# Down projections of both feed-forward parts with activations stationary and 512 weight columns moving

## What is computed

```python
# first block, end
h = rmsnorm(x, g_pre_mlp)
f = square(relu(h @ w_up))          # 2048 -> 8192
f = f @ w_down                      # 8192 -> 2048
x = x + rmsnorm(f, g_post_mlp)
# second block: mixers, cross attention, then
u = rmsnorm_2(h, ffn_norm_w)
h = h + square(relu(u @ ffn_w1)) @ ffn_w2
return rmsnorm_2(h, final_norm_w)   # x * rsqrt(mean(x*x) + 1e-6) * w, per token
```

## Time and profile before

| | us |
|---|---|
| median of three runs | 2883.87 |
| lowest, highest | 2883.01, 2886.10 |
| the profiled execution | 2884.09 |
| its span, first to last instruction | 2882.3 |

### The profile page before, as it was taken

How to read it: one execution, slowest core, us unless ns; L and a number is a source line. 1 busy time by engine, 2 the same in 40 slices (tenths; PEclk the granted TensorE clock), 3 DMA queues, 4 the chain that set the end, 5 groups by cost and what they waited for, 6 DMA issues and landing times.

```text
span 2882.3 us, 51300 instructions
## 1 busy us (share of the span) xinstructions
PE 2807.8 (97%) x19504; PEld 2458.9 (85%) x19504; DVE 2005.7 (70%) x2465; ACT 1440.9 (50%) x1867; POOL 158.3 (5%) x173
## 2 busy tenths in 40 slices
PE   9999999999999999999998999889989999999998
PEld 8888888888888888888787888788878888888887
DVE  7888887768647566575887667855877666575665
ACT  6545556566444444445656437434654444444444
POOL 0000000230000000001000000131220000000001
PEclk9999999999999999999999999999999999999999
DMA  7565554756666666656464434402536665656664
GB/s 245 175 194 163 169 175 152 231 176 208 189 188 188 190 188 187 188 184 194 133 196 118 133 111 125 125 4 75 183 118 207 189 188 189 190 186 189 187 189 139
DMA packets 482034, 486.70 MB, mean 169 GB/s; under 512 B 14945, under 2 KB 479841, under 8 KB 481873
## 3 DMA queue, kind: packets, MB, share of 16 engines
q1 hardware_dynamic: 480288, 478.55, 53.7%
q0 software_dynamic: 1584, 5.93, 0.6%
HBM read 481.28 MB, written 3.15 MB: 168 GB/s over the span
## 4 chain that ended last, share of the span: by engine, by line
PE 88%; DVE 7%; ACT 3%; issue 2%; DMA 0%; SPq 0%; DVEq 0%; ACTq 0%
PE pg L430 53%; PE pg L437 28%; DVE lo L348 1%; PE p L1082 1%; DVE work L795 1%; PE p L1099 1%; DVE xa L656 1%; ACT hi L310 1%; PE p L1510 0%; PE pg L1780 0%; DMA resid<-x 0%; DVE work L773 0%; PE p L1259 0%; PE p L1102 0%; PE p L1077 0%
## 5 line engine op out<-in xcount | busy, mean ns | idle before, releaser
L348 DVE TENSOR_TENSOR lo<-raw,hi 128x1024 fp32r<-128x1024 f32 x895 | 1086.3, 1232 | 646.2 <-ACT hi L310 640.0
L310 ACT ACTIVATE hi<-raw 128x1024 fp32r<-128x1024 f32 x894 | 939.0, 1059 | 1128.7 <-PE pg L437 1064.4
L430 PE MATMUL pg<-xa,hi 128*128 128x512 f32 x4224 | 1070.6, 395 | 7.2 <-DVE xa L656 3.8
L430 PEld LDWEIGHTS pg<-xa,hi 128*128 128x128 f32 x4224 | 761.7, 189 | 149.5 <-issue 6.3
L430 PE MATMUL pg<-xb,hi 128*128 128x512 f32 x3004 | 755.5, 393 | 3.8 <-ACT hi L310 1.9
L430 PEld LDWEIGHTS pg<-xb,hi 128*128 128x128 f32 x3004 | 541.3, 189 | 102.8 <-issue 2.9
L437 PEld LDWEIGHTS pg<-xa,lo 128*128 128x128 f32 x4224 | 576.3, 191 | 52.8 <-DVE lo L348 11.1
L437 PE MATMUL pg<-xa,lo 128*128 128x256 f32 x4224 | 591.6, 283 | 5.5 <-DVE lo L348 4.7
L437 PEld LDWEIGHTS pg<-xb,lo 128*128 128x128 f32 x3004 | 409.5, 190 | 34.1 <-DVE lo L348 5.1
L437 PE MATMUL pg<-xb,lo 128*128 128x256 f32 x3004 | 419.4, 282 | 3.0 <-DVE lo L348 3.0
L320 ACT ACTIVATE half<-pg 128x512 f32<-128x512 f32 x220 | 128.6, 585 | 77.5 <-PE pg L437 70.9
(11 more groups left out here) (422 smaller groups left out, 1681.1 us busy)
## 6 DMA issues: line engine op xcount, KB each, us to landing
raw<-w_in SPq DMA_DIRECT2D x264, 512.0 KB, 4.5
raw<-ffn_w SPq DMA_DIRECT2D x256, 512.0 KB, 4.3
raw<-w_up SPq DMA_DIRECT2D x128, 512.0 KB, 3.9
raw<-w_down SPq DMA_DIRECT2D x128, 512.0 KB, 4.5
raw<-w_o SPq DMA_DIRECT2D x32, 512.0 KB, 4.6
raw<-w_out SPq DMA_DIRECT2D x32, 512.0 KB, 4.5
raw<-w_sb_out SPq DMA_DIRECT2D x16, 512.0 KB, 4.7
raw<-w_conv_out SPq DMA_DIRECT2D x16, 512.0 KB, 4.7
```

Source lines behind the costliest of these rows:

```text
L310: nc.scalar.activation(hi[:, slot], raw[:, slot], ACT.Copy).then_inc(hi_ready, 1)
L348: nc.vector.tensor_tensor(lo[:, slot], raw[:, slot], hi[:, slot].bitcast(F32), ALU.subtract).then_inc(lo_ready, 1)
L430: nc.tensor.matmul(pg[:, par, t, :], lhsT=hi[:, slot, k, c:c + P], rhs=g.x[:, kk, :], start=(j == 0 and k == 0), stop=False)
```

## The change

The eight down projections (`down0` to `down3`, `w2_0` to `w2_3`) get a new kind, "tokens". Their slabs hold 2 tiles of the contraction by 512 columns; a block is 512 output features in 8 slabs, and there are 4 blocks. The activations become the stationary operand: for each of 2 tiles and 2 halves of the tokens, TensorE runs one matmul with the high activations and one with the low ones against 512 columns of `hi`, then one with the high activations against `lo`. All three sums meet in the same PSUM bank, so ScalarE copies nothing, and VectorE moves or adds 1024 elements a block into `acc` (`work` tiles 32 to 47), whose rows are tokens.

- The squares behind `down3` and `w2_3` are sums along a row: `Square` with a running sum on ScalarE, a small reduction, root and reciprocal per partition.
- Behind `down3`, VectorE scales the identity by the reciprocals (`token_diag`); TensorE multiplies tiles of `acc` with it, which transposes and scales them; VectorE adds each, times its weight, to `resid`. All four quarters of this stand in TensorE's queue ahead of `g_dn`, with matmuls of `warm` between them.
- `w2` accumulates in `acc`, not in `resid`; therefore during `w1_0` TensorE transposes `resid` in four groups of eight, and ScalarE copies them into `acc`.
- At the end ScalarE and VectorE scale rows by the per-partition reciprocal; the final weights come as a broadcast 1 MB tile that GpSimd loads earlier, and VectorE multiplies by it beside the last blocks. The output is written with rows that are tokens. GpSimd's sums of squares for the two norms and `token_root_pe` are gone.

```diff
-        self.groups = k // (P * KG)
-        self.blocks = n // BW
+        self.tokens = kind in ("tokens", "tokens add")
+        self.kg, self.bw = (KG // 2, 2 * BW) if self.tokens else (KG, BW)
+        self.groups = k // (P * self.kg)
+        self.blocks = n // self.bw
...
-            down = Gemm(plan, f"down{p}", a["w_down"], D, 0, D, xb, "add" if p else "store", (work, 16, PAD), k0=p * D)
+            down = Gemm(plan, f"down{p}", a["w_down"], D, 0, D, xb, "tokens add" if p else "tokens", (acc, 0, PAD), k0=p * D)
...
+            if g.tokens:
+                dve.wait_ge(slab_used, g.slab(i, v, g.groups - 1)[2] + 1 + RING)
+                place = into[:, :, bass.ds(2 * t, 2), off:off + BW]
+                sums = pg[:, par].rearrange("p t (n c) -> p t n c", n=2)
+                if g.kind == "tokens":
+                    nc.vector.tensor_copy(place, sums).then_inc(evacuated, 1)
+                else:
+                    nc.vector.tensor_tensor(place, place, sums, ALU.add).then_inc(evacuated, 1)
+                return
...
+        def tokens_slab(pe, g, par, j, slot, s):
+
+            first, last = j == 0, j == g.groups - 1
+            for k in range(g.kg):
+                for t in range(2):
+                    for part in range(2):
+                        c = part * T + t * P
+                        nc.tensor.matmul(pg[:, par, t, :], lhsT=g.x[:, j * g.kg + k, c:c + P], rhs=wide(hi[:, slot])[:, k],
+                                         start=(first and k == 0 and part == 0), stop=False)
+            pe.wait_ge(lo_ready, s + 1 + RING)
+            for k in range(g.kg):
+                for t in range(2):
+                    ins = nc.tensor.matmul(pg[:, par, t, :], lhsT=g.x[:, j * g.kg + k, t * P:(t + 1) * P],
+                                           rhs=wide(lo[:, slot])[:, k], start=False, stop=(last and k == g.kg - 1))
+            ins.then_inc(slab_used, 1)
...
-                        pe.wait_ge(evacuated, of.b0 + KG // 2 * (j + 1) + 2)
+                        pe.wait_ge(evacuated, of.b0 + g.kg // 2 * (j + 1) + 2)
...
+        def token_squares(m):
+            for t in range(2):
+                y = YS + 4 * m + 2 * t
+                ins = nc.scalar.activation(work[:, y:y + 2, PAD:COLS], acc[:, t, 2 * m:2 * m + 2, PAD:COLS], ACT.Square,
+                                           accum_out=xm[:, 4 * t + m:4 * t + m + 1])
+            return ins
...
+        def acc_turn_pe(pe, q):
+            pe.wait_ge(norm_used, DT * 4)
+            if q >= 2:
+                wait_added(pe, 1, q - 2)
+            for n in range(4):
+                for t in range(2):
+                    o, c = n % 2 * T + t * P, PAD + n % 2 * P
+                    ins = nc.tensor.matmul(turned_bank(q)[:, n // 2, o:o + P], lhsT=acc[:, t, 2 * q + n // 2, c:c + P],
+                                           rhs=token_diag[:, t], start=True, stop=True)
+            ins.then_inc(acc_turned, 1)
...
+        def resid_turn_pe(pe):
+
+            for q in range(4):
+                if q >= 2:
+                    pe.wait_ge(acc_added, q - 1)
+                for t in range(2):
+                    for n in range(4):
+                        ins = nc.tensor.transpose(turned_bank(q)[:, t, n * P:(n + 1) * P], resid[:, 4 * q + n, t * P:(t + 1) * P],
+                                                  const("ident"))
+                ins.then_inc(acc_turned, 1)
+                yield from skip(3)
...
             for g, n in zip(ff1, ff1[1:] + [g_dn]):
                 gemm_dve(dve, g, follows=n, left=1 if n is g_dn else 0, each=step_of(up_fold()) if g is ff1[0] else None)
+            split_lo_one(dve, g_dn, 3)
             token_inverse_dve(dve, 3)
-            y_scale_dve(dve, 1, 0, 3)
-            y_add_dve(dve, 1, 0)
+            token_diag_dve(dve)
+            acc_add_dve(dve, 0, post_mlp_w)
             for q in range(1, 4):
-                y_scale_dve(dve, 1, q, 3)
-                if q == 1:
-                    split_lo_one(dve, g_dn, 3)
+                acc_add_dve(dve, q, post_mlp_w)
                 next_dve(dve, 2, q - 1, mix_w)
-                y_add_dve(dve, 1, q)
             next_dve(dve, 2, 3, mix_w)
...
-            token_root_pe(pe, 3, 5, 11)
+            pe.wait_ge(consts_in, 16)
+            warm(8)
+            for q in range(4):
+                acc_turn_pe(pe, q)
+                if q:
+                    warm(4, pg[:, 0, 0])
...
+            token_std_act(act, ff2[-1], 7)
+            norm_rs_dve(act, 7)
+            act.wait_ge(out_weighted, 4)
+            for h in range(2):
+                x = outs[:, 0, 4 * h:4 * h + 4, PAD:COLS]
+                nc.scalar.activation(x, x, ACT.Copy, scale=token_inv[:, 0:1]).then_inc(out_act, 1)
```

More of the change, by code:

```diff
@@ L96, in __init__ @@
         plan.slabs += self.blocks * self.groups
-        plan.sums += self.blocks if kind != "store" else 0
+        plan.sums += self.blocks if kind != "store" and not self.tokens else 0
         plan.squares += self.blocks if kind == "relu2" else 0
@@ L128, in __init__ @@
     def __init__(self):
-        self.blocks = self.slabs = self.sums = self.squares = 0
+        self.blocks = self.slabs = self.sums = self.squares = self.halves = 0
         self.stages = []
@@ L263, in run_blocks, with wide @@
                     after(whole * unroll + v)
+        def wide(slab):
+            return slab.rearrange("p (a b) n -> p a (b n)", b=2)
         def load_weights(sp, g, part=0):
@@ L579, in norm_total, with warm @@
             nc.tensor.matmul(ps[0][:, 0:T], lhsT=const("ones"), rhs=sq_sum[:, :], start=True, stop=True).then_inc(norm_sum, 1)
-        token_std, token_inv = small[:, 136:138], small[:, 138:140]
-        root_row = ps[2][:, 0:T]
-        def warm(n):
+        xm = small[:, 120:136]
+        token_tot, token_std, token_inv = small[:, 128:130], small[:, 136:138], small[:, 138:140]
+        def warm(n, bank=None):
             for _ in range(n):
-                nc.tensor.matmul(ps[3][:, 0:T], lhsT=const("ones"), rhs=cst[:, 0:2], start=True, stop=True)
@@ L610, in token_std_act @@
-        def token_std_act(act, n):
-            act.wait_ge(token_sum, BY_TOKEN.index(n) + 1)
-            nc.scalar.activation(token_std[:, :, None], p4[:, 0:2, 0:1], ACT.Sqrt, scale=1.0 / D, bias=EPS).then_inc(token_sd, 1)
-        def token_inverse_dve(dve, n):
-            dve.wait_ge(token_sd, BY_TOKEN.index(n) + 1)
-            nc.vector.reciprocal(token_inv, token_std).then_inc(token_inverse, 1)
+                nc.tensor.matmul(ps[3][:, 0:T] if bank is None else bank[:, 0:T], lhsT=const("ones"), rhs=cst[:, 0:2], start=True, stop=True)
@@ new lines, in token_squares, with token_beside_act, after @@
+        def token_squares(m):
[4 more added lines that the diff above has]
+            return ins
+        def token_beside_act(act, g):
+            def after(m):
+                if m:
+                    act.wait_ge(evacuated, g.b0 + m + 2)
+                    token_squares(m - 1)
+                if m == g.blocks - 1:
+                    if g is ff1[-1]:
+                        split_hi_one(act, g_dn, 2)
+                    act_link(nc.scalar.activation(small[:, 140:141], const("ones")[:, 0:1], ACT.Sqrt))
+            return after
@@ L729, in y_scale_dve @@
             dve.wait_ge(y_weighted, DT * e + 4 * q + 4)
[L730 removed]
+            root = rs
             nc.vector.tensor_tensor(y4(q), y4(q), root[:, None, :].to_broadcast([P, 4, T]), ALU.mult).then_inc(y_ready, 1)
```

170 lines of the change are left out of this document (97 added, 73 removed).

## The result

| | before | after |
|---|---|---|
| median of 4 runs, us | 2883.70 | 2866.35 |
| lowest, highest | 2883.01, 2886.10 | 2864.62, 2867.11 |
| ratio, 95% interval | | 0.9938, 0.9925 to 0.9951 |
| span of the profiled execution | 2882.3 | 2865.3 |

The change makes the kernel 17.35 us faster, 0.6%. The prediction was 2869.0 with 2861 to 2886; the measured time lies inside it, and the sign was right. The rest asks whether it was right for its reasons.

The account below looks back on a forecast made before the run. TensorE bounds the kernel, busy 2807.8 of 2882.3 us. Slab -17.7, turning the residual +3.7, seam +0.6 and end -1.5 sum to -14.9 us, taking 2884.1 to 2869, range 2861 to 2886.

Parts of the forecast that it names:

- The slab: Down-projection slabs: 12 wide matmuls at 227 ns instead of 16 mixed, 69 ns less a slab, -17.7 us over 256 slabs.
- a debt to the narrow ones: Old slab: 256 columns barely cover loading the next stationary tile; the next five wide matmuls pay, 232 against 227 ns.
- Moving operand: Down slabs: spacing with ring slabs as moving operand, taken as 227 ns, bounded by 216 (-51 us) and 241 (+26 us).
- Rival 2: Down slabs: streaming from ring slabs beside those being written slows matmuls to 241 ns, giving 2913 us; 14%.
- rival 4: Down slabs: the 227 ns belong to the old moving tile and fall to 216, giving 2836 us; 5%.
- Rival 1: Down slabs: some 8 ns a matmul independent of width, so only -7.7 us there and 2879 in all; 18%.
- Order of VectorE: First down block: VectorE splits 8 slabs before the last up evacuation; hidden with 2.0 us to spare, 0.
- Rival 3: Down pieces: the last up evacuation ends too late, each of 8 pieces waits 1 us, giving 2877; 5%.
- Turning the residual: First w1 piece: four groups of 8 transposes paid in full on TensorE, 0.93 us each, +3.7 us.
- Seam: After down3: TensorE's own queue sets it; g_dn starts at 16.7 us, its sixth slab about 31.0, +0.6 us.
- End: After the last matmul: first output transfer issued at 4.7 us against 6.2, -1.5 us.
- Clock: Between the feed-forward parts: stretches at half clock may fall on other work; 3 us allowed either way.

Follow-up runs that it names:

- the narrow matmuls put back: Changed kernel with each 512-column low-weight matmul of the down projections issued as two of 256 columns again; 2886.10 us, ratio 1.0009 to the kernel before.
- the gathered rows: Changed kernel with every second up-projection slab taking low weights first, so 16 wide matmuls follow 16 narrow ones; 2865.89 us, ratio 0.9936.
- the uneven halves: Changed kernel, but each 512-column low-weight matmul of the down projections issued as 384 and 128 columns; 2934.74 us, ratio 1.0177.
- the second run: Kernel before, each 512-column high-weight matmul followed at once by the 256-column low-weight one of the same tile; 2917.08 us, ratio 1.0107.

## Why the prediction was right, and where it was off

**The slab.** The step that carried the sum held in mechanism and size: 69 ns a slab forecast, 73 measured (the rounding of 226.7 to 227 and of 2.793), 17.7 and 18.6 us. The reading that the last three of eight wide matmuls show the true price, and the first five a debt to the narrow ones before them, was confirmed by the narrow matmuls put back and the gathered rows; the uneven halves show the floor under the narrow ones. That the next tile's load is that floor is still only argued. What fell is my extension of it in the second run: I expected wide and narrow matmuls in turn to be free of the debt, and it is paid at every change from narrow to wide.

**Moving operand.** No cost: 227 ns a matmul with the ring slabs moving, within 1 ns over each phase. Rival 2 (slower) and rival 4 (216 ns) are out; the spacing is the old settled one. The fixed 2.5 ns a matmul and 216 ns for 512 columns that the Trainium skill has ("TensorE: Matmul & The Clock Gate", "Wait — 56ns, not 53.3ns?") fit neither kernel's fp32r matmuls. Rival 1, the fixed cost, is out by the uneven halves.

**Order of VectorE.** Hidden, as worked out. In `down0` slab 7 of TensorE starts at 783.40; the last operation of the last `up` evacuation:

```profile
780.36 0.69 DVE L421 TENSOR_TENSOR xb<-sq,xb 128x512 fp32r<-128x512 f32 x1
...
783.40 1.98 PE L443 MATMUL pg<-hi,xb 128*128 128x512 f32 x8
```

It ends 2.35 us before (2.0 forecast). Rival 3 is out.

**Turning the residual.** 3.7 forecast, 3.5 in the trace, 3.5 by the trace of the run without it (4.1 by its median).

**Seam.** +0.6 forecast, +0.2 measured. The path was right, TensorE's own queue. The first turn starts at 1384.67, 4.0 us behind 1380.68 and not 4.3, because the two diagonal scalings take 0.5 us together where the sum had 0.7; and the 12 keep-busy matmuls between the turns take 5.0 us and not 5.2. VectorE's additions also came out shorter, 0.43 us each (3.45 for eight at 1386.76) and not 0.484, but they lie beside the path.

**End.** -1.5 forecast, -0.8 measured. The step that failed is the count of what stands in VectorE's queue. The sum goes from the evacuation and ScalarE's squares straight to the reduction, and puts VectorE's products with the final weights at nothing. One product of 1.2 us behind the evacuation would have hidden behind the squares, but two stand there: `final_beside` runs one block late, so the third product comes behind the last evacuation as well as the fourth. Moving the third gave the 0.7 us back.

**Clock.** The 3 us allowed either way cover what came: +1.6 and -2.8.

**The number.** In spans, 14.9 us were forecast and 17.0 came. The slab (1.0 more), the turning (0.2), the seam (0.4) and the clock (1.2) came out better, the end (0.7) worse. The forecast lies so near because its largest term was right; that the clock's two shares partly cancelled was luck.

## What to carry to other kernels

Give an fp32r matmul that brings its own stationary tile the full 512 columns: here those of 256 took 119 ns and not 113, and slowed the wide ones behind them, so that equal columns in fewer, wider matmuls were worth 2.6% of this stream. Read single start times before settling on a price; the mean over a phase hid the two levels on which the forecast rests. At a seam, count every instruction in each engine's queue, keep-busy matmuls and late callbacks included, and keep only as many of the former as hold the clock. Here that was one group of 8 in front of the first turn; a smaller one wasn't tried.

## What was not expected of the hardware

- Wide and narrow matmuls in turn are dearer (353 ns a pair) than the same in rows of 8 (2.793/8 = 349) or of 16 (5.57/16 = 348), and all are dearer than their columns at the settled price (340).
- A running sum on ScalarE is a second instruction: 0.62 us for the squares of 512 elements and 0.19 us to read the sum. It starts before the squares end, so that two such pairs take 1.34 us (1382.13 to 1383.47).
- VectorE's scaling of 128 x 1024 by a column takes 0.71 us (1.42 for two at 2856.22), ScalarE's of the same shape 1.1, where VectorE's sum of two such tensors takes 1.22.
- Stretches at half clock come and go in kernels that are the same up to there. Near 484 us TensorE is busy throughout at half clock in the kernel after, and not in the one before. Both have two waits of TensorE shortly ahead of it, of 1.53 us (to 472.8) and of 2.1 us (to 482.5, for a low split of VectorE), and so have the experiments, of which some show the stretch and others don't. No run here shows what decides it; differences of 1 to 3 us between versions of this kernel have to be read with the stretches of their traces.
